# Attention heads taken in pairs: one step of lag, VectorE's divisions and maxima ahead of the weight split, and four biases with places of their own

## The chip, the cores and the metric

The kernel runs on one core of one Trainium2 chip. The metric is the device time of one execution in microseconds (us), given as the median over runs; one further execution was recorded by the profiler.

## The reference

One layer of a hybrid encoder over 512 tokens of width 2048, in float32: a combined input projection, three groups of mixers side by side (A: 8 heads of chunked attention with a relative bias, B: RWKV-7, C: 8 heads of sliding-window attention with sinks), an output projection, a cross-attention into 256 memory tokens, an MLP of width 8192, and a last norm. What the change touches are the attentions of A and C:

```python
logits = jnp.einsum('bcqhd,bckhd->bchqk', qc, kb).astype(jnp.float32) * (d ** -0.5)
logits = logits + bias[None, None]
logits = jnp.where(valid[None, :, None, None, :], logits, NEG_INF)
p = jax.nn.softmax(logits, axis=-1).astype(v.dtype)
o = jnp.einsum('bchqk,bckhd->bcqhd', p, vb)
```

In C the softmax has one more column, the sink of the head. The heads have 64 features, the chunks 64 tokens; A sees its own chunk and 8 before it (here: all earlier keys), C its own and one before it.

## The kernel before

Nearly all the work is a product of activations with weights on TensorE. Both sides are split into a high and a low part of type fp32r, and `split_mm` makes three products (L1176 to L1178) of each. A "unit" is two tiles of 128 rows of weights: SyncE loads it into one of four slots of `w_raw`, ScalarE copies it to `w_hi` (`hi_next`), VectorE subtracts to `w_lo` (`lo_next`, which raises `w_split`), and there are two slots of the split parts. So while TensorE works at unit n, ScalarE and VectorE make unit n + 1. A unit is 8 places of 3 products; `side(i)` puts other work of TensorE ahead of place i.

The attentions lie in the units v = 4 to 31 of three groups of products: the keys and values of the cross-attention (`G_XK`, `G_XV`, v = 0 to 15, products of 256 columns), and the part of the output projection that takes RWKV's output (`G_WR`, v = 16 to 31, 512 columns). The next group (`G_WA`, v = 32 on) takes the attentions' output and waits for all of it (`o_lo` of 8). At the end of v = 7, 15, 19, 23, 27 and 31 VectorE takes finished banks out of PSUM (`scaled_by_row`, `add_set`), and TensorE waits for it at the next unit.

Before, a unit of attention n (64 of them) is a tile t of two heads (t 0 to 3: A, t 4 to 7: C), one of its heads (`half`, features in partitions 0 to 63 or 64 to 127), and a block i of 128 queries. It has 128 (i + 1) keys in A and 128 or 256 in C: 136 blocks of 128 keys in all. It goes through a pipeline, one step each: TensorE makes the scores (L1386); VectorE adds the bias and takes the maximum (`sc_max`, L1000) and negates it (`sc_neg`, L1007 or L1010); ScalarE takes the exponential and its sum (`p_exp`, L610); VectorE divides (`p_ready`, L988 and L990); TensorE turns the blocks of 128 x 128 (`pT_mm`, L1395); ScalarE copies them to `att_pT` (`pT_ev`); TensorE multiplies with the values (`o_mm`, L1407). When the 8 units of a tile are done, ScalarE copies the tile (`o_hi`) and VectorE subtracts (`o_lo`, L1017). Scores, turning and outputs are products of type float32, which the profile shows as two passes each for scores and outputs.

Every engine runs the steps in one order written out by hand, and the units v say which steps are in each of them:

```python
def att_steps(v):
    if v < 4:
        return []
    steps_ = [2 * (v - 4) + i for i in range(2)] if v < 16 else [24 + 3 * (v - 16) + i for i in range(3)]
    return [st for st in steps_ if st < N_UNITS_ATT + 3]
```

GpSimd loads, in one order for all tiles, the queries and keys of a tile (`qk`), and the bias of each head n = 2t + half (L420), which it then masks with MEMSETs (`bias_ready`). Ahead of bias 1 it waits for the norm of the memory and loads RWKV's output `y_in` into h; ahead of bias 5 it waits until VectorE has split the eight tiles of `y_in` (`y_lo`, one in each unit v = 4 to 11, L1054), and then loads x into h, 1 MB at a time (L415).

Of the kernel before, what the change touches and what calls it, by code (L numbers as in the profile page):

```python
# [23 lines left out]
P = 128  # L24
# [3 lines left out]
L = 64  # L28
# [26 lines left out]
N_UNITS_ATT = 64  # L55
# [7 lines left out]
def hybrid_layer(nc, x, x_turned, mem_turned, gains, w_lora, w_pairs, w_rest, pair_prm, fin_prm, gup_tail, lora_mu,  # L63
                 a_line, c_line, sinks, norm_final, out):
    top = ExitStack()
    with top:
# [192 lines left out]
        def unit_of(n):  # L259
            t, half, i = n // 8, (n // 4) % 2, n % 4  # L260
            return (("A", t, half, i) + a_window(i)) if n < 32 else (("C", t, half, i) + c_window(i))
# [42 lines left out]
        def _(pool):  # L304
# [92 lines left out]
            for t in range(8):  # L397
                qt, kt = (t, 4 + t) if t < 4 else (A_TILES + t - 4, A_TILES + 4)
                if t >= 2:
                    pool.wait_ge(s["sc_mm"], 8 * (t - 1))  # L400
                pool.dma_start(qk[:, t % 2, 0, :], scr_qkv[qt // 3, qt % 3]).then_inc(s["qk_in"], 16)
                pool.dma_start(qk[:, t % 2, 1, :], scr_qkv[kt // 3, kt % 3]).then_inc(s["qk_in"], 16)
                for half in range(2):
# [16 lines left out]
                    pool.dma_start(bias[:, n % 2, 0:w], hankel).then_inc(s["bias_in"], 16)  # L420
                    pool.wait_ge(s["bias_in"], 16 * (n + 1))

                    step(nc.gpsimd.memset(bias[0:L, n % 2, 0:L], MASKED))
                    if t >= 4:
                        step(nc.gpsimd.memset(bias[0:L, n % 2, w - L:w], MASKED))
                        step(nc.gpsimd.memset(bias[L:P, n % 2, P:w], MASKED))
# [8 lines left out]
        def _(act):  # L435
# [152 lines left out]
            hi(0, UNITS * G_IN // RAW + 1, rest_slot(w_hi, 0), UNITS * G_IN)  # L588
            def att_step(st):
                n = st - 2  # L590
                if 0 <= n < N_UNITS_ATT:
                    keys = unit_of(n)[5]
                    act.wait_ge(s["pT_mm"], n + 1)
                    if n >= 2:
                        act.wait_ge(s["o_mm"], n - 1)
                    copy(att_pT[:, n % 2, 0:keys], ps[:, 6, 0:keys]).then_inc(s["pT_ev"], 1)
                n = st - 3
                if n >= 0 and n % 8 == 7:
                    t = n // 8
                    act.wait_ge(s["o_mm"], n + 1)  # L600
                    copy(act_hi[:, t if t < 4 else t + 8, :], bank(7)).then_inc(s["o_hi"], 1)
                n = st
                if n < N_UNITS_ATT:
                    kind, t, half, i, key0, keys = unit_of(n)
                    act.wait_ge(s["sc_neg"], n + 1)
                    if kind == "C":
                        head = (t - 4) + 4 * half
                        nc.scalar.activation(att_c[:, n % 4, 3:4], sink[:, head:head + 1], ACT.Exp,
                                             bias=att_c[:, n % 4, 1:2])
                    nc.scalar.activation(att_p[:, n % 4, 0:keys], att_p[:, n % 4, 0:keys], ACT.Exp,  # L610
                                         bias=att_c[:, n % 4, 1:2],
                                         accum_out=att_c[:, n % 4, 2:3]).then_inc(s["p_exp"], 1)
# [107 lines left out]
        def _(dve):  # L720
# [258 lines left out]

            def att_step(st):  # L980
                n = st - 1
                if 0 <= n < N_UNITS_ATT:
                    kind, keys = unit_of(n)[0], unit_of(n)[5]
                    dve.wait_ge(s["p_exp"], n + 1)
                    if kind == "C":
                        V.tensor_tensor(att_c[:, n % 4, 2:3], att_c[:, n % 4, 2:3], att_c[:, n % 4, 3:4], ALU.add)
                        dve.drain()
                    V.reciprocal(att_c[:, n % 4, 0:1], att_c[:, n % 4, 2:3])  # L988
                    dve.drain()
                    V.tensor_scalar(att_p[:, n % 4, 0:keys], att_p[:, n % 4, 0:keys], att_c[:, n % 4, 0:1], None,  # L990
                                    ALU.mult).then_inc(s["p_ready"], 1)
                n = st
                if n < N_UNITS_ATT:
                    kind, t, half, i, key0, keys = unit_of(n)
                    hd = n // 4
                    dve.wait_ge(s["sc_mm"], n + 1)
                    dve.wait_ge(s["bias_ready"], hd + 1)
                    if n >= 4:
                        dve.wait_ge(s["pT_mm"], n - 3)
                    V.tensor_tensor_reduce(out=att_p[:, n % 4, 0:keys], in0=ps[:, 4 + n % 2, 0:keys],  # L1000
                                           in1=falling(bias[:, hd % 2, 0:keys]), scale=1.0, scalar=-3e38,
                                           op0=ALU.add, op1=ALU.max,
                                           accum_out=att_c[:, n % 4, 0:1]).then_inc(s["sc_max"], 1)
                    dve.wait_ge(s["sc_max"], n + 1)
# [635 lines left out]
```

## Time and profile before

| | us |
|---|---|
| three runs, median (lowest to highest) | 2751.24 (2750.96 to 2754.89) |
| profiled execution, its time | 2754.32 |
| span of the profiled execution | 2752.6 |
| TensorE busy in it | 2715.1 |
| VectorE, ScalarE, GpSimd busy | 1238.5, 816.0, 133.6 |

The span goes from the first to the last instruction. "Busy" of TensorE counts matmuls from issue to a modelled end, so they overlap: of two that follow each other, the time between the starts is the cost, not the duration printed. TensorE's clock was granted at 0.997 of full on average.

### The profile page before, as it was taken

Reading aid. Unit: us, or ns where it says so; the run is one execution under the profiler, and the core shown is the slowest. Engines: PE = TensorE matmul, PEld = TensorE weight load, DVE = VectorE, ACT = ScalarE, POOL = GpSimd, SP = SyncE. Lnnn points to the kernel's source line nnn. Section 1 sums busy time; section 2 is a strip of 40 time slices with the busy share of each in tenths; the row PEclk is TensorE's granted clock in tenths of the full one; section 3 lists DMA queues with packets and bytes.
Section 4 is the critical chain, followed back from the end, with each engine's and each line's share of the span. In section 5 each row is a group of like instructions: output and inputs, shape, how many; then the busy total and the mean of one; then the engine's idle time right before and its main releaser. Section 6 shows DMA issues by size and latency. Waiting matters only on the chain.

```text
span 2752.6 us, 44358 instructions
## 1 busy us (share of the span) xinstructions
PE 2715.1 (99%) x18368; PEld 2159.3 (78%) x18368; DVE 1238.5 (45%) x1916; ACT 816.0 (30%) x1340; POOL 133.6 (5%) x237
## 2 busy tenths in 40 slices
PE   9999999999999999998999999999999999999997
PEld 7877777777777766786888888888888888888886
DVE  6266666666435545344433333333333333324334
ACT  5222222222125444344432222322222222122233
POOL 4000111001121100000000000000000000000000
PEclk9999999999999999999999999999999999999999
DMA  4311111111235521221223222222223222222232
GB/s 167 120 55 49 48 48 51 45 48 49 62 102 204 180 70 61 85 92 62 91 93 100 98 94 99 96 94 99 94 96 99 93 98 99 92 98 93 98 100 100
DMA packets 72403, 249.33 MB, mean 91 GB/s; under 512 B 8960, under 2 KB 9088, under 8 KB 71104
## 3 DMA queue, kind: packets, MB, share of 16 engines
q1 hardware_dynamic: 65232, 222.62, 24.6%
q0 software_dynamic: 7024, 24.56, 2.7%
q8 instruction: 115, 1.88, 0.3%
q14 instruction: 32, 0.26, 0.0%
HBM read 236.93 MB, written 10.22 MB: 90 GB/s over the span
## 4 chain that ended last, share of the span: by engine, by line
PE 97%; DVE 1%; ACT 1%; issue 0%; DMA 0%; DVEq 0%; ACTq 0%; SPq 0%
PE ps L1176 28%; PE ps L1178 26%; PE ps L1177 26%; PE ps L1194 9%; PE ps L1407 1%; PE ps L1386 1%; PE ps L1395 1%; PE ps L1188 1%; PE ps L1246 0%; PE ps L1243 0%; PE ps L1226 0%; PE ps L1237 0%; DVE w_lo L725 0%; PE ps L1252 0%; PE ps L1221 0%
## 5 line engine op out<-in xcount | busy, mean ns | idle before, releaser
L725 DVE TENSOR_TENSOR w_lo<-w_raw,w_hi 128x1024 fp32r<-128x1024 f32 (+2 forms) x440 | 505.9, 1150 | 1136.4 <-ACT w_hi L437 1136.3
L437 ACT ACTIVATE w_hi<-w_raw 128x1024 fp32r<-128x1024 f32 (+2 forms) x440 | 438.9, 998 | 1537.5 <-PE ps L1178 1537.1
L1176 PE MATMUL ps<-act_hi,w_hi 128*128 128x512 f32 x1792 | 730.5, 408 | 1.9 <-DVE w_lo L725 1.9
L1178 PE MATMUL ps<-act_hi,w_lo 128*128 128x512 f32 x1792 | 700.7, 391 | 0.0
L1177 PE MATMUL ps<-act_lo,w_hi 128*128 128x512 f32 x1792 | 700.1, 391 | 0.0
L1176 PE MATMUL ps<-w_hi,mid_hi 128*128 128x512 f32 x1088 | 425.1, 391 | 3.9 <-DVE w_lo L725 2.5
L1177 PE MATMUL ps<-w_lo,mid_hi 128*128 128x512 f32 x1088 | 424.0, 390 | 0.0
L1178 PE MATMUL ps<-w_hi,mid_lo 128*128 128x512 f32 x1088 | 423.9, 390 | 0.0
L1176 PEld LDWEIGHTS ps<-act_hi,w_hi 128*128 128x128 f32 x1792 | 336.5, 188 | 94.8 <-issue 12.1
L1178 PEld LDWEIGHTS ps<-act_hi,w_lo 128*128 128x128 f32 x1792 | 336.8, 188 | 72.3
L1177 PEld LDWEIGHTS ps<-act_lo,w_hi 128*128 128x128 f32 x1792 | 337.0, 188 | 69.2 <-issue 6.0
L1176 PEld LDWEIGHTS ps<-w_hi,mid_hi 128*128 128x128 f32 x1088 | 204.6, 188 | 46.6 <-DVE w_lo L725 2.9
L1178 PEld LDWEIGHTS ps<-w_hi,mid_lo 128*128 128x128 f32 x1088 | 204.6, 188 | 42.6
L1177 PEld LDWEIGHTS ps<-w_lo,mid_hi 128*128 128x128 f32 x1088 | 204.6, 188 | 42.0
L1030 DVE SCALAR_TENSOR_TENSOR h<-ps,rq,h 128x512 f32<-128x512 f32 x124 | 84.5, 743 | 96.4 <-PE ps L1178 96.4
L1176 PE MATMUL ps<-w_hi,act_hi 128*128 128x512 f32 x256 | 106.3, 415 | 4.2 <-DVE h L1024 3.6
L1178 PE MATMUL ps<-w_hi,act_lo 128*128 128x512 f32 x256 | 100.2, 392 | 0.0
L1177 PE MATMUL ps<-w_lo,act_hi 128*128 128x512 f32 x256 | 100.1, 391 | 0.0
L1176 PEld LDWEIGHTS ps<-w_hi,act_hi 128*128 128x128 f32 x256 | 48.0, 187 | 21.5 <-issue 13.3
L1178 PEld LDWEIGHTS ps<-w_hi,act_lo 128*128 128x128 f32 x256 | 48.0, 188 | 10.8
L1177 PEld LDWEIGHTS ps<-w_lo,act_hi 128*128 128x128 f32 x256 | 48.2, 188 | 8.1
L1176 PE MATMUL ps<-mid_hi,w_hi 128*128 128x256 f32 (+1 forms) x144 | 46.0, 319 | 3.3 <-DVE w_lo L725 2.7
(283 smaller groups left out, 2409.0 us busy)
## 6 DMA issues: line engine op xcount, KB each, us to landing
w_raw<-in_w_rest SPq DMA_DIRECT2D x320, 512.0 KB, 3.3
w_raw<-in_w_pairs SPq DMA_DIRECT2D x112, 384.0 KB, 3.0
x_t<-in_x_turned SPq DMA_DIRECT2D x8, 512.0 KB, 8.4
qk<-scr_qkv POOLq DMA_DIRECT2D x16, 256.0 KB, 3.1
h<-in_x POOLq DMA_DIRECT2D x4, 1024.0 KB, 11.4
out<-h SPq DMA_DIRECT2D x4, 1024.0 KB, 3.9
scr_qkv<-pad POOLq DMA_DIRECT2D x15, 256.0 KB, 4.1
w_raw<-in_w_lora SPq DMA_DIRECT2D x8, 288.0 KB, 7.3
```

Of the source, the lines that this page charges most:

```text
L437: return nc.scalar.activation(dst, src, ACT.Copy, scale=scale)
L725: V.tensor_tensor(dst, w_raw[:, slot, 0:dst.shape[-1]], high.bitcast(F32), ALU.subtract).then_inc(s["w_split"], 1)
L1030: V.scalar_tensor_tensor(dst, bank(4 * par + t), rq[:, 1, t:t + 1], dst, ALU.mult, ALU.add).then_inc(s["bank_evac"], 1)
L1176: mm(dst, a_hi, b_hi, start=start, stop=False)
L1177: mm(dst, a_hi, b_lo, start=False, stop=False)
L1178: return mm(dst, a_lo, b_hi, start=False, stop=stop)
L1188: last = nc.tensor.transpose(ps[:, turn_bank(k, kt), t * P:(t + 1) * P], h[:, t, kt * P:(kt + 1) * P], ident[:, :])
L1194: last = mm(dst[hf], lhsT[hf], rhs[hf], start=start, stop=stop)
L1386: mm(ps[:, 4 + n % 2, 0:keys], qk[hf, t % 2, 0, i * P:(i + 1) * P], qk[hf, t % 2, 1, key0:key0 + keys], start=True, stop=True).then_inc(s[ ...
L1395: last = nc.tensor.transpose(ps[:, 6, b * P:(b + 1) * P], att_p[:, n % 4, b * P:(b + 1) * P], ident[:, :])
L1407: last = mm(ps[HALF[half], 7, i * P:(i + 1) * P], vt[:, key0 // P + b, v0:v0 + L], att_pT[:, n % 2, b * P:(b + 1) * P], start=b == 0, stop ...
```

## The change

The unit of work is now a pair: the two heads of a tile for one block of queries, 32 of them, in 33 steps with one step of lag instead of three. In a step TensorE makes the scores of pair st and turns and multiplies pair st - 1, in four parts at four places of a unit. The two heads of the scores are issued one behind the other, on rows 0 to 63 and 64 to 127 of the array, into two banks; the outputs of the two heads take turns block by block, on columns 0 to 63 and 64 to 127. ScalarE takes exponentials of the new pair and copies of the old one in turn. VectorE does the divisions of the old pair and the maxima of the new pair, and in each unit the first step stands ahead of the split of the next unit. The biases 2 to 5 lie in h[:, 1], the biases 8, 9, 14 and 15 in `diag`, the others in `bias`; x's second block is loaded later, ahead of bias 8.

```diff
-            steps_ = [2 * (v - 4) + i for i in range(2)] if v < 16 else [24 + 3 * (v - 16) + i for i in range(3)]
-            return [st for st in steps_ if st < N_UNITS_ATT + 3]
+            steps_ = [v - 4] if v < 23 else [2 * v - 27, 2 * v - 26] if v < 28 else [v + 1]
+            return [st for st in steps_ if st <= ATT_PAIRS]
...
+        def bias_of(hd):
+            if hd < 8:
+                return bias[:, hd % 2, :] if hd // 2 in (0, 3) else h[:, 1, (hd - 2) * A_KEYS:(hd - 1) * A_KEYS]
+            near = diag[:, :, :].rearrange("p t n -> p (t n)") if hd // 2 in (4, 7) else bias[:, hd // 2 - 5, :]
+            return near[:, hd % 2 * C_KEYS:(hd % 2 + 1) * C_KEYS]
...
                     if n == 5:
                         pool.wait_ge(s["y_lo"], PAIRS)
                         pool.wait_ge(s["row_ready"], 2)
-                        for i in range(TT):
+                        for i in (0, 2, 3):
                             pool.dma_start(h[:, i, :], x[i * P:(i + 1) * P, :]).then_inc(s["h_in"], 16)
-                    if n >= 2:
-                        pool.wait_ge(s["sc_max"], 4 * (n - 1))
+                    if n == 8:
+                        pool.wait_ge(s["sc_max"], 24)
+                        pool.dma_start(h[:, 1, :], x[P:2 * P, :]).then_inc(s["h_in"], 16)
+                        pool.wait_ge(s["bank_evac"], 4 * (S_XV + 1))
+                    if t in (3, 5, 6, 7):
+                        pool.wait_ge(s["sc_max"], {3: 8, 5: 32, 6: 32, 7: 40}[t])
...
             def att_step(st):
+                for half in range(2):
+                    if st < ATT_PAIRS:
+                        att_exp(st, half)
+                    if st:
+                        att_turned(st - 1, half)
+                n = st - 1
+                if n >= 0 and n % 4 == 3:
+                    t = n // 4
                     act.wait_ge(s["o_mm"], n + 1)
                     copy(act_hi[:, t if t < 4 else t + 8, :], bank(7)).then_inc(s["o_hi"], 1)
...
             def att_step(st):
+                if st:
+                    for half in range(2):
+                        att_divide(st - 1, half)
+                if st < ATT_PAIRS:
+                    for half in range(2):
+                        att_max(st, half)
                 n = st - 1
+                if n >= 0 and n % 4 == 3:
+                    t = n // 4
                     mt = t if t < 4 else t + 8
                     dve.wait_ge(s["o_hi"], t + 1)
...
                     v = UNITS * (g - G_XK) + u
-                    lo_next(g, u)
+                    todo = att_steps(v) if g < G_WA else []
+                    for st in todo:
+                        att_step(st)
+                        if st == todo[0]:
+                            lo_next(g, u)
+                    if not todo:
+                        lo_next(g, u)
...
+                for half, hf in enumerate(HALF):
+                    last = mm(ps[:, 4 + half, 0:keys], qk[hf, t % 2, 0, i * P:(i + 1) * P],
+                              qk[hf, t % 2, 1, key0:key0 + keys], start=True, stop=True)
+                last.then_inc(s["sc_mm"], 1)
...
+                for b in range(nb):
+                    for half, hf in enumerate(HALF):
+                        v0 = t * P + half * L if kind == "A" else 512 + half * L
+                        last = mm(ps[hf, 7, i * P:(i + 1) * P], vt[:, key0 // P + b, v0:v0 + L],
+                                  att_pT[:, half, b * P:(b + 1) * P], start=b == 0, stop=b == nb - 1)
+                last.then_inc(s["o_mm"], 1)
...
-                        for j, st in enumerate(todo):
-                            if i == (8 * j + 4) // len(todo):
-                                att_step(st)
+                        if len(todo) == 1 and i % 2 == 1:
+                            att_part(todo[0], i // 2)
+                        elif len(todo) == 2:
+                            att_part(todo[i // 4], i % 4)
```

On TensorE, in the units of 256 columns, one place of a unit before held scores (L1386), turning (L1395) and outputs (L1407) of three units of attention in a row, between products of the weights:

```order
L1178 MATMUL ps<-mid_hi,w_lo 128x256
L1386 MATMUL ps<-qk 128x384
L1395 MATMUL ps<-ident,att_p 128x128
L1407 MATMUL ps<-att_pT,vt 64x128 x4
L1176 MATMUL ps<-mid_hi,w_hi 128x256
```

Of the change, the second turning and the outputs of a pair (L1419, L1432; the products are L1201 to L1203 there), at places 5 and 7 of a unit:

```order
L1419 MATMUL ps<-ident,att_p 128x128
L1201 MATMUL ps<-mid_hi,w_hi 128x256
L1202 MATMUL ps<-mid_lo,w_hi 128x256
L1203 MATMUL ps<-mid_hi,w_lo 128x256
L1201 MATMUL ps<-mid_hi,w_hi 128x256
L1202 MATMUL ps<-mid_lo,w_hi 128x256
L1203 MATMUL ps<-mid_hi,w_lo 128x256
L1432 MATMUL ps<-att_pT,vt 64x128 x2
L1201 MATMUL ps<-mid_hi,w_hi 128x256
```

Each part now stands alone between products, and only one place of three products is left behind the outputs in a unit.

On VectorE, before, at the end of the first tile of heads, in unit 9 (`w_lo` is the split, L1054 the split of `y_in`, L1017 the low part of the tile's output):

```order
L725 TENSOR_TENSOR w_lo<-w_raw,w_hi 128x1024
L1054 TENSOR_TENSOR act_lo<-h,act_hi 128x512
L988 RECIPROCAL att_c<-att_c 128x1
L990 TENSOR_SCALAR att_p<-att_p,att_c 128x256
L1000 ISA att_p,att_c<-ps,bias 128x384
L1000 ISA att_c 128x1
L1010 TENSOR_SCALAR att_c<-att_c 128x1
L1017 TENSOR_TENSOR act_lo<-ps,act_hi 128x512
```

Of the change, at the end of the same tile, in unit 8 (L1015 and L1024 are maximum and negation, L1038 the low part of the output, L742 the split, L1081 that of `y_in`):

```order
L1005 TENSOR_SCALAR att_p<-att_p,att_c 128x512
L1015 ISA att_p,att_c<-ps,h 128x128
L1015 ISA att_c 128x1
L1024 TENSOR_SCALAR att_c<-att_c 128x1
L1015 ISA att_p,att_c<-ps,h 128x128
L1015 ISA att_c 128x1
L1024 TENSOR_SCALAR att_c<-att_c 128x1
L1038 TENSOR_TENSOR act_lo<-ps,act_hi 128x512
L742 TENSOR_TENSOR w_lo<-w_raw,w_hi 128x1024
L1081 TENSOR_TENSOR act_lo<-h,act_hi 128x512
```

The split has moved from the head of a unit to behind the tile's output.

On GpSimd, before, biases 4 and 5 and the loads of x between them:

```order
L401 DMA qk<-scr_qkv 128x512
L402 DMA qk<-scr_qkv 128x512
L420 DMA bias<-in_a_line 128x512
L423 MEMSET bias 64x64
L415 DMA h<-in_x 128x2048 x4
L420 DMA bias<-in_a_line 128x512
L423 MEMSET bias 64x64
```

Of the change, the same place:

```order
L410 DMA qk<-scr_qkv 128x512
L411 DMA qk<-scr_qkv 128x512
L433 DMA h<-in_a_line 128x512
L436 MEMSET h 64x64
L424 DMA h<-in_x 128x2048 x3
L433 DMA h<-in_a_line 128x512
L436 MEMSET h 64x64
```

Bias 5 (the second of tile t = 2) keeps its place behind the loads of x, of which there are three instead of four. Its first use was step 20, in unit 14; by pairs it is step 8, in unit 12.

## Rows read from the trace of the kernel before

**Rows 1.** The page: busy us, share of the span, number of instructions.

```profile
PE 2715.1 (99%) x18368; PEld 2159.3 (78%) x18368; DVE 1238.5 (45%) x1916; ACT 816.0 (30%) x1340; POOL 133.6 (5%) x237
```

**Rows 2.** Windows: stretch, length, busy of each engine, granted clock, DMA share, GB/s.

```profile
873.20:1121.49 248.29, 242.01 (x1207) 165.22 (x1206) 128.07 (x418) 108.56 (x270) 21.58 (x61) 1.00 0.31 102
```

**Rows 3.** Timeline of TensorE: start, duration, engine, line, operation, count.

```profile
906.97 0.91 PE L1386 MATMUL ps<-qk 64*128 64x384 f32 x2
907.81 0.33 PE L1395 MATMUL ps<-ident,att_p 128*128 128x128 f32 x1
908.07 1.09 PE L1407 MATMUL ps<-att_pT,vt 128*64 128x128 f32 x8
909.09 0.38 PE L1176 MATMUL ps<-mid_hi,w_hi 128*128 128x256 f32 x1
...
909.55 0.28 PE L1176 MATMUL ps<-mid_hi,w_hi 128*128 128x256 f32 x1
...
968.30 1.12 PE L1386 MATMUL ps<-qk 64*128 64x512 f32 x2
969.35 0.44 PE L1395 MATMUL ps<-ident,att_p 128*128 128x128 f32 x2
969.72 0.43 PE L1407 MATMUL ps<-att_pT,vt 128*64 128x128 f32 x2
970.08 0.50 PE L1176 MATMUL ps<-w_hi,act_hi 128*128 128x512 f32 x1
```

**Rows 4.** Timeline of TensorE, two products of 64 rows (RWKV's part).

```profile
141.12 0.39 PE L1178 MATMUL ps<-act_hi,w_lo 128*128 128x512 f32 x1
141.44 0.69 PE L1221 MATMUL ps<-lora,prm 64*128 64x512 f32 x1
141.45 0.69 PE L1222 MATMUL ps<-lora,prm 64*128 64x512 f32 x1
141.98 0.59 PE L1221 MATMUL ps<-lora,prm 64*128 64x512 f32 x1
...
142.50 0.50 PE L1176 MATMUL ps<-act_hi,w_hi 128*128 128x512 f32 x1
142.84 0.39 PE L1177 MATMUL ps<-act_lo,w_hi 128*128 128x512 f32 x1
```

**Rows 5.** Timeline of TensorE, four turned blocks alone between products.

```profile
1175.89 0.40 PE L1178 MATMUL ps<-w_hi,act_lo 128*128 128x512 f32 x1
1176.13 0.60 PE L1188 MATMUL ps<-ident,h 128*128 128x128 f32 x4
...
1176.80 0.39 PE L1177 MATMUL ps<-w_lo,act_hi 128*128 128x512 f32 x1
```

**Rows 6.** Timeline of VectorE: the split, a maximum and its negation, a tile's low part.

```profile
921.39 1.23 DVE L725 TENSOR_TENSOR w_lo<-w_raw,w_hi 128x1024 fp32r<-128x1024 f32 x1 [2.26 <-ACT w_hi L437]
...
923.64 0.55 DVE L1000 CUSTOM_DVE_ANT_0 att_p<-ps,bias 128x384 f32<-128x384 f32 x1
...
924.23 0.15 DVE L1010 TENSOR_SCALAR att_c<-att_c 128x1 f32<-128x1 f32 x1
...
937.58 0.69 DVE L1017 TENSOR_TENSOR act_lo<-ps,act_hi 128x512 fp32r<-128x512 f32 x1
```

**Rows 7.** Groups by line, ScalarE, 860 to 1120: busy, mean ns, idle before.

```profile
L437 ACT ACTIVATE act_hi<-ps 128x512 fp32r<-128x512 f32 x8 | 4.8, 599 | 6.1 <-PE ps L1407 6.1
```

**Rows 8.** Timeline of GpSimd, and the landing of its x loads.

```profile
923.51 2.12 POOL L415 DMA_DIRECT2D h<-in_x  x4 [6.31 <-DVE act_lo L1054]
...
941.64 0.15 POOL L423 MEMSET bias<- 64x64 f32 x1 [14.35 <-DMA bias<-in_a_line]
...
DMA to landing us min/median/max: 7.8/11.4/15.7
```

**Rows 9.** Windows, columns as in rows 2, about TensorE's gap ahead of unit 0.

```profile
854.48:857.15 2.67, 0.00 (x1) 0.03 (x1) 2.34 (x4) 2.00 (x2) 2.67 (x6) 1.00 0.73 233
857.50:861.50 4.00, 4.00 (x24) 4.00 (x23) 0.53 (x1) 0.70 (x1) 1.10 (x3) 0.57 0.94 338
```

More of the change, by code:

```diff
@@ L588, in _, with att_turned @@
             hi(0, UNITS * G_IN // RAW + 1, rest_slot(w_hi, 0), UNITS * G_IN)
-            def att_step(st):
[L590 to L599, printed above, removed]
+            def att_turned(n, half):
+                keys = unit_of(n)[4]
+                act.wait_ge(s["pT_mm"], 2 * n + half + 1)
+                if n:
+                    act.wait_ge(s["o_mm"], n)
+                copy(att_pT[:, half, 0:keys], ps[:, 6, 0:keys]).then_inc(s["pT_ev"], 1)
@@ new lines, in att_exp @@
+            def att_exp(n, half):
+                kind, t, i, key0, keys = unit_of(n)
+                j = slot_of(n, half)
+                act.wait_ge(s["sc_neg"], 2 * n + half + 1)
+                if kind == "C":
+                    head = (t - 4) + 4 * half
+                    nc.scalar.activation(att_c[:, j, 3:4], sink[:, head:head + 1], ACT.Exp, bias=att_c[:, j, 1:2])
+                nc.scalar.activation(att_p[:, j, 0:keys], att_p[:, j, 0:keys], ACT.Exp, bias=att_c[:, j, 1:2],
+                                     accum_out=att_c[:, j, 2:3]).then_inc(s["p_exp"], 1)
@@ L603, in att_step @@
[L603 to L612, printed above, removed]
@@ L978, in _ @@
             lo(UNITS * G_IN, 0, rest_slot(w_lo, 0), rest_slot(w_hi, 0))
-            def att_step(st):
-                n = st - 1
[L982 to L1004, printed above, removed]
-                    if kind == "C":
-                        head = (t - 4) + 4 * half
-                        V.tensor_scalar(att_c[:, n % 4, 1:2], att_c[:, n % 4, 0:1], sink[:, head:head + 1], -1.0,
-                                        ALU.max, ALU.mult).then_inc(s["sc_neg"], 1)
-                    else:
-                        V.tensor_scalar(att_c[:, n % 4, 1:2], att_c[:, n % 4, 0:1], -1.0, None,
-                                        ALU.mult).then_inc(s["sc_neg"], 1)
-                n = st - 3
-                if n >= 0 and n % 8 == 7:
-                    t = n // 8
@@ new lines, in att_turn @@
+            def att_turn(n, half):
+                keys = unit_of(n)[4]
+                pe.wait_ge(s["p_ready"], 2 * n + half + 1)
+                if 2 * n + half:
+                    pe.wait_ge(s["pT_ev"], 2 * n + half)
+                for b in range(keys // P):
+                    last = nc.tensor.transpose(ps[:, 6, b * P:(b + 1) * P],
+                                               att_p[:, slot_of(n, half), b * P:(b + 1) * P], ident[:, :])
+                last.then_inc(s["pT_mm"], 1)
@@ new lines, in att_out @@
+            def att_out(n):
+                kind, t, i, key0, keys = unit_of(n)
+                pe.wait_ge(s["pT_ev"], 2 * n + 2)
+                if n % 4 == 0 and t:
+                    pe.wait_ge(s["o_lo"], t)
+                nb = keys // P
+                for b in range(nb):
[4 more added lines that the diff above has]
+                last.then_inc(s["o_mm"], 1)
@@ L1412, in rest_unit, with att_part @@
+            def att_part(st, part_):
+                if part_ == 0 and st < ATT_PAIRS:
+                    att_scores(st)
+                elif part_ in (1, 2) and st:
+                    att_turn(st - 1, part_ - 1)
+                elif part_ == 3 and st:
+                    att_out(st - 1)
             def rest_unit(n, u, stationary, a_hi, a_lo, kts, cols, par, first, last_kt, reused, side=None, turned_out=None):
```

91 lines of the change are left out of this document (45 added, 46 removed).

## The prediction

> **What bounds the kernel now.** I read the page first: TensorE is busy for 99% of the span [rows 1], so only work taken off TensorE, or waits of TensorE, can move the end. Then the windows answer for the stretch of the attentions, units 4 to 31, from the first score to the first product of the stage behind: 248.3 us, TensorE busy 242.0, idle 6.3, clock at full, VectorE busy 128 and ScalarE 109 of it [rows 2]. So VectorE and ScalarE have room on average, and the rest is read unit by unit. The timeline of TensorE in two units [rows 3] gives the parts of an attention step. Scores of 512 keys take 1.05 us to the next start, of 384 keys 0.84: 0.21 per 128 keys and 0.20 fixed. Turning a block costs 0.11 (0.26 for one, 0.37 for two) and 0.15 fixed. The outputs cost 0.11 per pass, two passes per block (1.02 for eight passes, 0.36 for two), and 0.14 fixed. What the products lose at the two ends of such a group is seen at [rows 4]: 0.32 instead of 0.23 ahead of it and 0.34 instead of 0.23 behind it, 0.20 together.
>
> **The change, part by part.** *Work on TensorE.* The 64 units of before have 136 blocks of 128 keys. Now each unit costs 0.20 + 0.15 + 0.14 + 0.20 = 0.69 fixed and 0.21 + 0.11 + 0.21 = 0.53 per block: 64 x 0.69 + 136 x 0.53 = 44 + 73 = 117 us.
>
> The change issues the scores of two heads back to back, one on rows 0 to 63 of the array and one on 64 to 127. The trace has this very shape: L1221 and L1222 start at 141.44 and 141.45, again at 141.98, and the four passes of 512 columns end after 1.06 us [rows 4], as long as two passes of one head take now (1.05). So a pair of scores costs what one costs. The scores stand alone between products, so a pair pays 0.20 + 0.20 fixed. The turned blocks are as many, but stand alone too: four of them between two products (1175.89, 1176.13, 1176.80) stretch 0.91 - 0.45 = 0.46, 0.11 each with nothing fixed [rows 5]. The outputs of a pair go to columns 0 to 63 and 64 to 127, with different moving data. No row shows that form. Bounds: overlapped fully, 0.21 per block of the pair; not at all, 0.42. I take full overlap, because its nearest row is the row pair [rows 4], also two halves of the array with two moving operands; fixed 0.14 + 0.20.
>
> New sum, 32 pairs with 68 blocks: fixed 32 x (0.40 + 0.34) = 24, per block 0.21 + 0.22 + 0.21 = 0.64, 44 us: 68. TensorE loses 117 - 68 = 49 us of work (35 if the outputs don't overlap).
>
> The Trainium skill, "TensorE: Matmul & The Clock Gate", "Measured speedup vs the span model", gives 2.38x for three column tiles, below the factor 3; an estimate by that, 1.6x for two tiles, would cost 3 to 4 us of the 49. The same page says in "The mechanism" that matmuls start and end in strict order; with both passes of one half ahead of the other half's that would be three slots for a pair of scores instead of two, 7 us more. The rows show two slots [rows 4], so I leave it out.
>
> *The order on VectorE: the split waits for the output of a tile.* The next unit's `w_lo` now stands behind all of the first step of a unit. In a plain unit this is hidden: with scores three products into the unit (0.4 us) and ready 0.9 later, two maxima at 0.75 each (923.64 to the end of 924.23's row, 0.74 [rows 6]) and `w_lo` (1.2 [rows 6]) end at about 4.1, while the shortest unit lasts 24 products x 0.12 (0.36 for three: 0.46 from 909.09 to 909.55, less the 0.10 behind a group [rows 3]) + 0.74 + one to four blocks, 4.5 to 6.5. Margin 0.4 to 2.
>
> But at a step that ends a tile (st a multiple of 4) VectorE first waits for `o_hi`, which waits for the outputs, and these are issued at place 7 of 8, ahead of the unit's last three products. From the start of the outputs of four blocks: 0.85 + 0.30 to their end, ScalarE's copy 0.60 [rows 7], `act_lo` 0.6 to the next start and `w_lo` 1.23 [rows 6], with hand-overs of 0.1: 3.7 us. TensorE in that time has 0.85 + 0.34 + 0.36 = 1.55. So TensorE waits 2.1 us. That is at units 8 and 12; with three products of 512 columns (0.69) it is 1.8 at units 16 and 20. In units 23, 25 and 27 the ending step is the second of the unit, behind the split, and only delays the adding of the set by 0.3. At unit 31 `o_lo`, then the split, then the first addition to h stand in a row: 2.4 us, 1.5 more than now. Sum 8 + 2 = 10 us.
>
> *The order on GpSimd: bias 5 behind x.* This is the largest term. The four biases let 2, 3 and 4 be loaded early, but bias 5 (heads counted as n = 2t + half) still stands behind the wait for all eight `y_lo` and behind the loads of x. Now it is needed at unit 14; by pairs it is needed at step 8, unit 12, and the eighth `y_lo` is done in unit 11. Now the x loads start at 923.51, bias 5 is there at 941.64 after a wait of 14.35, and the four x loads land 7.8 to 15.7 us after their issue, in steps of 3 us: the third so at about 937.5 [rows 8], the bias some 0.8 behind it, 0.1 to 0.2 more for its masking. With three loads ahead, bias 5 comes about 14.5 us after their start. `y_lo` ends about 1.1 us before unit 12 begins (unit 11: split done at 4.4, then 0.7, of 6.2). So bias 5 is there 13.4 us into unit 12. VectorE's second maximum waits for it, ScalarE's second exponential for that, and the copy of the second turned half (and so TensorE's outputs at place 7) stands behind that exponential: 13.4 + 0.5 + 0.5 + 0.5 = 14.9 against 4.1 without it. TensorE waits 10.8 us. Bounds: nothing, if the bias passed the x loads; 13, if it came with the end of four (18.1 us).
>
> *Chain of a step.* Half 1 is turned when ScalarE has copied half 0, six products earlier. Copies of three or four blocks (0.5 to 0.6) and an exponential ahead of them make waits of 0.1 to 0.3 at about twelve pairs and about 1 at the four where steps follow in a two-step unit or first meet 512 keys: 7 us, an estimate, against 1.5 to 2 of the 6.3 now; the rest of those stays (evacuated banks). Bounds 2 and 12.
>
> *The clock.* Behind a gap of 2.67 us (TensorE busy 0.00 from 854.48 to 857.15) the mean granted clock of 857.5 to 861.5 is 0.57 [rows 9]: between the two levels, 1.2 and 2.4 GHz, that is 3.4 us at the lower one, 1.7 us lost. The gap of 11 us will surely do that, for 2.5 us with the wait behind it; of the five of about 2 us I count one or two, 2.5 us. Bounds 2 and 11.
>
> Sum: -49 + 10 + 11 + 5 + 5 = -18 us. Terms rounded the other way (117.7 - 69.2 = 48.5, 34 - 6.7 = 27.3 of waits) give -16; I take -17. The profiled execution took 2754.3 us, 3.1 above the median of the three runs, so 2737.3 there and 2734 for the median.
>
> **The rivals.**
> *A. The outputs don't overlap by columns.* For it: no row has the form, and both halves need all 128 rows. Against: [rows 4]. It gives 14 us back: 2748, no change that can be told. Chance 0.17. The change not doing what it says (pairs one after another) ends at the same place.
> *B. The bias is no wait.* For it: three loads may land much faster than four did, if the split weights ask for less at that time. Against: it waited 14.35 us in just this place [rows 8]. 11 + 2.5 us less: 2721. Chance 0.12.
> *C. Slower: the split is late in every plain unit.* VectorE's `w_lo` ends at 4.1 into units of 4.5 and up. If the divisions at the head wait for the last exponential, each microsecond beyond the margin costs TensorE a microsecond per unit. There are 23 such units; with a mean margin of 1.5 (more in the units of 512 columns) the kernel is slower than before by more than 0.2% from 2.5 us of delay per unit on, since 17 + 5.5 us over 23 units is 1.0 beyond the margin. For it: margins of 0.4 and 1 in units 4 and 5. Against: VectorE has 5 us of work in a unit of 6.5 and more. At 1.1 us per unit: -17 + 25 = +8, 2759. Chance 0.09.
>
> **How the numbers follow.** Forecast, between 2727 and 2743: 0.60. A 0.17, B 0.12, C 0.09, elsewhere 0.02. A measurement of this kernel tells 0.2%, 5.5 us, from no change. Faster: forecast 0.60, B 0.12 and a small part of A 0.03, in all 0.75. Same: the rest of A, 0.14. Slower: C and the rest, 0.11. The range goes down past B's 2721 by 3 us of a cheaper clock, 2718, and up past A's 2748 to 2750; C lies outside. The forecast's own range, 2727 to 2743, is its sum with the bounds of chain and clock.
>
> **What would show it.** Right: score pairs starting together, with as much time as one; outputs of a pair at 0.21 per block; one TensorE gap of about 11 us near 60 us after the first score, with GpSimd waiting for the bias; gaps of 1.8 to 2.4 behind `act_lo` at the ends of tiles 0, 1, 2, 3 and 7; the stretch from first score to the next stage near 230 us instead of 248. Wrong: outputs at 0.42 per block, no gap at bias 5, or `w_lo` ending behind TensorE in units that end no tile.

## The result, and the profile after

The changed kernel takes 2736.73 us (median of 5 runs, 2734.98 to 2740.60), the kernel before 2752.57 beside it: a ratio of 0.9944, 95% interval [0.9934, 0.9955]. That is 0.56% faster; forecast were 2734 us, from 2718 to 2750, and faster. One of the five executions of the kernel before took 4457.83 us and the other four 2750.96 to 2754.89, with a median of 2751.91, so the gain is 15 to 16 us. The profiled execution took 2739.77 us, 3.0 above the median, with a span of 2738.0.

TensorE is still the bound. The page has it busy for 37.5 us less than in [rows 1], though the span is only 14.6 us shorter, so waits have come in (busy us, share of the span, instructions):

```profile
PE 2677.6 (98%) x18368; PEld 2139.4 (78%) x18368; DVE 1235.5 (45%) x1916; ACT 811.9 (30%) x1340; POOL 133.0 (5%) x237
```

The windows answer for the stretch from the first score to the next stage, and for three pieces of it (busy us of PE, PEld, DVE, ACT and POOL with instructions, granted clock, DMA share, GB/s):

```profile
871.57:1107.01 235.44, 205.17 (x1206) 145.66 (x1206) 125.11 (x418) 104.59 (x270) 20.62 (x60) 0.94 0.33 104
...
920.00:940.00 20.00, 8.14 (x50) 6.26 (x48) 3.47 (x12) 3.41 (x8) 2.42 (x6) 0.62 0.60 223
940.00:1000.00 60.00, 56.24 (x336) 40.76 (x335) 29.25 (x91) 25.20 (x59) 6.93 (x22) 0.98 0.36 110
1000.00:1105.00 105.00, 96.56 (x492) 62.95 (x492) 56.27 (x210) 45.03 (x138) 6.23 (x20) 0.97 0.23 71
```

Beside [rows 2] the stretch is 12.9 us shorter by the windows and 12.4 from the first score's own start (247.8 before, 235.4 now). TensorE's busy time fell from 242.0 to 205.2, its idle time rose from 6.3 to 30, and its clock is no longer full. What it waits for stands in the list of TensorE's waits over the whole execution (us in total, times, longest), with four of its lines. Of the first, 4 waits and 6.9 us lie in the stretch, behind tiles 0 to 3; the other three lines lie in it altogether:

```profile
PE ps L1201 <- DVE w_lo L742: 12.9, 7, 2.7
PE ps L1432 <- ACT att_pT L450: 10.2, 1, 10.2
...
PE ps L1201 <- DVE h L1045: 5.0, 4, 2.4
PE ps L1419 <- ACT att_pT L450: 5.0, 11, 1.3
```

The 10.2 us are bias 5. GpSimd's timeline shows the three x loads, the bias load behind them, and 11.43 us until that has landed; TensorE's shows the gap, which ends 61 us after the first score (start, us, engine, line, operation, count, idle time before it and what ended it):

```profile
917.30 1.61 POOL L424 DMA_DIRECT2D h<-in_x  x3 [23.19 <-DVE act_lo L1081]
918.90 0.54 POOL L433 DMA_DIRECT2D h<-in_a_line  x1
930.88 0.14 POOL L436 MEMSET h<- 64x64 f32 x1 [11.43 <-DMA h<-in_a_line]
...
932.75 1.98 PE L1432 MATMUL ps<-att_pT,vt 128*64 128x128 f32 x16 [10.17 <-ACT att_pT L450]
```

The bias is there 13.6 us after the x loads' start. The outputs behind the gap last 1.98 us, against 1.09 for the same 16 passes at 997.92: the clock is at its lower level there.

The other new gap stands at the end of a tile. The timeline of all engines at the end of tile 0 (unit 8):

```profile
897.82 0.60 ACT L450 ACTIVATE act_hi<-ps 128x512 fp32r<-128x512 f32 x1 [1.19 <-PE ps L1432]
...
898.45 0.69 DVE L1038 TENSOR_TENSOR act_lo<-ps,act_hi 128x512 fp32r<-128x512 f32 x1 [3.40 <-ACT act_hi L450]
899.06 1.22 DVE L742 TENSOR_TENSOR w_lo<-w_raw,w_hi 128x1024 fp32r<-128x1024 f32 x1
...
900.33 0.39 PE L1201 MATMUL ps<-mid_hi,w_hi 128*128 128x256 f32 x1 [2.00 <-DVE w_lo L742]
```

From the last line up: TensorE has waited 2.00 us for the split, the split started when VectorE had the tile's low part, and VectorE had stood 3.40 us waiting for ScalarE's copy of the outputs, which came only after the outputs themselves.

**The balance of the stretch.** I counted TensorE's time from each start to the next, idle time left out, by line. Scores went from 41.9 to 22.2 us, turned blocks from 24.2 to 10.4, outputs from 39.0 to 20.8: 51.7 less. The weight products between them went from 136.5 to 152.2, 15.7 more. Marked gaps went from 6.3 to 29.8, 23.5 more. Together -12.5 (-12.4 before rounding). The 15.7 us in the products are more interesting than they look, since the trace calls them busy; the last two experiments take them apart.

### The profile page after: what moved, and what is told of

It is laid out like the page before. It is cut to its first block, busy times and chain, and to the rows that moved or that the text cites. A ratio compares the mean times of both kernels' runs of the same rounds, so it can differ in the third digit from the quotient of the medians.

```text
span 2738.0 us, 44362 instructions
## 1 busy us (share of the span) xinstructions
PE 2677.6 (98%) x18368; PEld 2139.4 (78%) x18368; DVE 1235.5 (45%) x1916; ACT 811.9 (30%) x1340; POOL 133.0 (5%) x237
## 4 chain that ended last, share of the span: by engine, by line
PE 94%; DVE 2%; ACT 1%; DMA 1%; issue 1%; DVEq 0%; POOL 0%; ACTq 0%; SPq 0%; POOLq 0%
PE ps L1201 28%; PE ps L1203 26%; PE ps L1202 26%; PE ps L1219 9%; PE ps L1432 1%; PE ps L1409 1%; PE ps L1419 1%; DMA h<-in_mem_turned 1%; PE ps L1213 1%; DMA h<-in_a_line 0%; DVE w_lo L742 0%; PE ps L1271 0%; PE ps L1262 0%; PE ps L1268 0%; PE ps L1251 0%
## 5 line engine op out<-in xcount | busy, mean ns | idle before, releaser
L742 DVE TENSOR_TENSOR w_lo<-w_raw,w_hi 128x1024 fp32r<-128x1024 f32 (+2 forms) x440 | 505.6, 1150 | 1076.0 <-ACT w_hi L450 1075.9
L1201 PE MATMUL ps<-act_hi,w_hi 128*128 128x512 f32 x1792 | 730.0, 407 | 0.8 <-DVE w_lo L742 0.8
L1203 PE MATMUL ps<-act_hi,w_lo 128*128 128x512 f32 x1792 | 700.0, 391 | 0.0
L1201 PE MATMUL ps<-w_hi,mid_hi 128*128 128x512 f32 x1088 | 425.3, 391 | 3.9 <-DVE w_lo L742 2.5
L1203 PE MATMUL ps<-w_hi,mid_lo 128*128 128x512 f32 x1088 | 423.8, 390 | 0.0
L1201 PEld LDWEIGHTS ps<-act_hi,w_hi 128*128 128x128 f32 x1792 | 336.1, 188 | 93.6 <-issue 12.1
L1203 PEld LDWEIGHTS ps<-act_hi,w_lo 128*128 128x128 f32 x1792 | 336.5, 188 | 72.2
L1201 PEld LDWEIGHTS ps<-w_hi,mid_hi 128*128 128x128 f32 x1088 | 204.6, 188 | 46.5 <-DVE w_lo L742 2.9
L1203 PEld LDWEIGHTS ps<-w_hi,mid_lo 128*128 128x128 f32 x1088 | 204.5, 188 | 42.7
L1201 PE MATMUL ps<-w_hi,act_hi 128*128 128x512 f32 x256 | 110.9, 433 | 8.9 <-DVE h L1045 5.0
L1203 PE MATMUL ps<-w_hi,act_lo 128*128 128x512 f32 x256 | 101.3, 396 | 0.0
L1201 PEld LDWEIGHTS ps<-w_hi,act_hi 128*128 128x128 f32 x256 | 48.8, 190 | 28.2 <-issue 15.7
L1203 PEld LDWEIGHTS ps<-w_hi,act_lo 128*128 128x128 f32 x256 | 48.8, 190 | 11.0
L1201 PE MATMUL ps<-mid_hi,w_hi 128*128 128x256 f32 (+1 forms) x144 | 49.5, 344 | 6.9 <-DVE w_lo L742 6.3
```

The source lines that it names most:

```text
L742: V.tensor_tensor(dst, w_raw[:, slot, 0:dst.shape[-1]], high.bitcast(F32), ALU.subtract).then_inc(s["w_split"], 1)
L1201: mm(dst, a_hi, b_hi, start=start, stop=False)
L1203: return mm(dst, a_lo, b_hi, start=False, stop=stop)
```

## The experiments

**1. Bias 5 ahead of the x loads.** GpSimd waits for `y_lo` and loads x one bias later.

```diff
-                    if n == 5:
+                    if n == 6:
                         pool.wait_ge(s["y_lo"], PAIRS)
```

> Bias 5 is loaded ahead of x's blocks 0, 2 and 3 instead of behind them; all else as in the change. My account (TensorE's gap of 10.2 us ahead of the outputs of pair 7 is the wait for bias 5, and the low clock behind it costs 3 us more): the gap is gone, the clock stays at full after unit 12, 12 to 13 us less than the change, near 2724 us. Rival (the gap is DMA traffic as such: any load at that time collides with the 3 MB of x): bias 6 or the queries and keys of tile 3, now behind x, are late instead, and a gap of 5 us or more stands near unit 16; at most 6 us less.

Measured: 2726.64 us (2725.83 to 2737.03), ratio 0.9902 [0.9885, 0.9919]: 10.1 us faster than the change, where 12 to 13 were expected and the rival allowed 6. The outputs' wait is gone from the list and no bias is late. But the clock did not stay at full: the profiled execution took 2737.03 us, 10 more than the other three, and no marked wait explains that. Its mean granted clock is 0.991, that of the other three 0.995 to 0.996. In its stretch the clock is low at the end of or behind each of the four gaps for `w_lo` and behind gaps of 1.51 and 1.30 us (1028.2), and once more right behind the stretch. Four windows of it:

```profile
870.00:920.00 50.00, 45.80 (x331) 37.37 (x330) 34.44 (x99) 30.46 (x66) 4.32 (x11) 0.93 0.42 135
920.00:940.00 20.00, 17.92 (x123) 14.58 (x122) 9.54 (x35) 8.46 (x20) 3.00 (x7) 0.83 0.71 263
940.00:1000.00 60.00, 54.64 (x303) 38.40 (x303) 29.83 (x91) 23.37 (x53) 6.84 (x21) 0.95 0.33 106
1000.00:1105.00 105.00, 96.26 (x489) 62.93 (x488) 55.96 (x202) 44.15 (x134) 6.58 (x21) 0.96 0.23 71
```

**2. The split ahead of a tile's low part.** VectorE issues `lo_next` before the part of a step that waits for `o_hi`.

```diff
                         att_step(st)
                         if st == todo[0]:
                             lo_next(g, u)
+                        att_tile_end(st)
```

> VectorE's low part of a finished tile (the wait for ScalarE's copy of it) is moved behind the next unit's split; maxima and divisions stay ahead of the split. My account: the waits of TensorE for w_lo of 2.0, 1.6, 1.7 and 1.7 us behind tiles 0 to 3 are gone, the one at unit 32 falls from 2.4 to about 1.3, and the low clock behind the 2.0 us gap (1.7 us) is gone: 8 to 9 us less than the change, near 2728 us. Rival (the split is late because of maxima and divisions ahead of it): the gaps stay above 1 us, 0 to 3 us less.

Measured: 2731.69 us (2728.59 to 2734.92), ratio 0.9920 [0.9904, 0.9937], 5.0 us faster than the change, not 8 to 9. The `w_lo` gaps at units 8, 12, 16 and 20 are gone and unit 32's is 1.22 instead of 2.36. Instead 0.81 us appear ahead of a turning, and the bias gap stays at 9.8. The cause of the waits is shown, and in the profiled execution so is their worth: its stretch is 9.9 us shorter than the change's (225.6 against 235.4), 7.7 of it marked gaps. Behind the stretch, where the two kernels are the same, it took 2.4 us longer, with a piece of low clock at 1266.5 that the change's profile has not.

**3. Both.**

> Both of the edits of the two runs ahead of this one. If the two waits are separate, the gains add up: 20 to 22 us less than the change, near 2716 us. If they share a cause, less than 16 us.

Measured: 2719.07 us (2713.23 to 2719.36), ratio 0.9876 [0.9859, 0.9892], 17.7 us faster than the change. Expected were 20 to 22 for separate waits and less than 16 for a shared cause, so the size lies between the two; but the single gains add up to 15.1, and both together gain no less than that, so the two waits are separate costs. The profiled execution was the fastest of the four, 2713.23. Its stretch, in the windows answer:

```profile
869.89:1081.98 212.09, 199.40 (x1207) 141.27 (x1206) 124.94 (x418) 104.24 (x270) 20.79 (x60) 0.98 0.37 118
```

**4. Outputs of the two heads one after the other**, all blocks of one half of the array's columns, then all of the other.

```diff
-                for b in range(nb):
-                    for half, hf in enumerate(HALF):
+                for half, hf in enumerate(HALF):
+                    for b in range(nb):
```

> The change, but the outputs of a pair are issued all blocks of the first head, then all of the second, so that two column halves are not in use at once except at the boundary. If the halves overlap by columns in the change: outputs of four blocks take near 1.9 us instead of 1.03, of two near 1.0 instead of 0.59, 0.21 us per block of a pair more, 68 blocks, up to 14 us in all (2749 us). If the saving came from fewer switches alone: no change.

Measured: 2740.94 us (2739.66 to 2744.84), ratio 0.9960 [0.9946, 0.9974], only 4.2 us slower than the change, where overlap alone was expected to cost up to 14. The outputs of two blocks still take 0.59 us, as in turn; three take 1.07 instead of 0.81, four 1.51 instead of 1.03. So this issue order keeps the halves apart only in part, and this run did not tell what overlap is worth. Numbers 6 and 7 do.

**5. The split ahead of the whole step**, the opposite of the change's order on VectorE.

```diff
-                    for st in todo:
-                        att_step(st)
-                        if st == todo[0]:
-                            lo_next(g, u)
-                    if not todo:
-                        lo_next(g, u)
+                    lo_next(g, u)
+                    for st in todo:
+                        att_step(st)
```

> The change with one part undone: in every unit VectorE makes the next unit's split first, as the kernel before does, and the divisions and maxima of the pair behind it. My account of why that order is there: with one step of lag the divisions must be done before place 3 of the unit, and the split waits for ScalarE's part, so TensorE would wait about 1 us at the turning of nearly every pair: 25 to 32 us more than the change, near 2765 us, slower than the kernel before; the gaps behind w_lo vanish. Rival (the order costs nothing but the gaps behind w_lo): 5 to 8 us less than the change.

Measured: 2777.00 us (2774.48 to 2778.43), ratio 1.0093 [1.0076, 1.0109]: 40 us slower than the change, more than the 25 to 32 expected, and slower than the kernel before. In the profile the stretch is 32.8 us longer than the change's, 24.5 of it marked gaps. TensorE's waits over the whole execution:

```profile
PE ps L1416 <- ACT att_pT L450: 22.4, 26, 1.4
PE ps L1416 <- DVE att_p L1005: 22.4, 23, 2.6
PE ps L1198 <- DVE w_lo L742: 7.0, 3, 2.7
```

The gaps for `w_lo` in the stretch are gone (the 7.0 lie outside it), and turnings wait instead, for divisions and copies. The lag of one step needs the divisions first; the split behind them makes no gap for `w_lo` where no tile ends, as the change and number 2 show.

**6 and 7. No overlap at all.** Number 6 takes experiment 4's loops and writes both heads' outputs to the same 64 columns; number 7 computes both score tiles on the same 64 rows.

```diff
-                        last = mm(ps[hf, 7, i * P:(i + 1) * P], vt[:, key0 // P + b, v0:v0 + L],
+                        last = mm(ps[HALF[0], 7, i * P:(i + 1) * P], vt[:, key0 // P + b, v0:v0 + L],
```

```diff
-                    last = mm(ps[:, 4 + half, 0:keys], qk[hf, t % 2, 0, i * P:(i + 1) * P],
-                              qk[hf, t % 2, 1, key0:key0 + keys], start=True, stop=True)
+                    last = mm(ps[:, 4 + half, 0:keys], qk[HALF[0], t % 2, 0, i * P:(i + 1) * P],
+                              qk[HALF[0], t % 2, 1, key0:key0 + keys], start=True, stop=True)
```

> The outputs of both heads of a pair go to columns 0 to 63 and the same place in PSUM, one head behind the other, so no two column halves can be in use at once; the second half of each attention output tile is not computed. If columns overlap in the change: outputs of two blocks take 1.0 us instead of 0.59, of four 1.9 instead of 1.03; 13 to 15 us more than the change, near 2751 us. If what mattered was the fewer switches: no more than 3 us.

> The scores of both heads of a pair are taken from the rows 0 to 63 (the first head's queries and keys twice; the second head's scores are not computed), so the two can't use two halves of the rows at once. If rows overlap in the change: a pair of scores of 512 keys takes 1.9 us instead of 1.06, of 256 keys 1.06 instead of 0.63; 13 to 15 us more than the change, near 2751 us, less where the gaps were. Rival: TensorE would overlap them whatever rows they use: no more than 3 us.

Measured: 2757.57 us (2754.61 to 2761.03, ratio 1.0017 [1.0007, 1.0027]) and 2757.08 (2754.83 to 2763.50, ratio 1.0019 [1.0010, 1.0029]): 20.8 and 20.4 us slower than the change. Each alone takes back the whole gain. TensorE's timeline, four blocks of outputs and the next product, in the change, in number 4 and in number 6:

```profile
997.92 1.09 PE L1432 MATMUL ps<-att_pT,vt 128*64 128x128 f32 x16
998.94 0.50 PE L1201 MATMUL ps<-w_hi,act_hi 128*128 128x512 f32 x1
```

```profile
999.99 1.58 PE L1432 MATMUL ps<-att_pT,vt 128*64 128x128 f32 x16
1001.50 0.50 PE L1201 MATMUL ps<-w_hi,act_hi 128*128 128x512 f32 x1
```

```profile
1008.70 1.96 PE L1432 MATMUL ps<-att_pT,vt 128*64 128x128 f32 x16
1010.59 0.50 PE L1201 MATMUL ps<-w_hi,act_hi 128*128 128x512 f32 x1
```

From start to next start 1.02, 1.51 and 1.89 us. One to four blocks take 0.37, 0.59, 0.81 and 1.03 in the change, 0.58, 1.02, 1.45 and 1.89 in number 6: 0.22 against 0.435 per block. And the scores of 512 keys in the change and in number 7, 1.06 against 1.91 to the next start:

```profile
982.47 1.13 PE L1409 MATMUL ps<-qk 64*128 64x512 f32 x4
983.53 0.50 PE L1201 MATMUL ps<-w_hi,act_hi 128*128 128x512 f32 x1
```

```profile
993.45 1.98 PE L1409 MATMUL ps<-qk 64*128 64x512 f32 x4
995.36 0.50 PE L1201 MATMUL ps<-w_hi,act_hi 128*128 128x512 f32 x1
```

By these rows 68 blocks times 0.21 are 14 to 15 us for either. Counted over the stretch of the profiled executions, from start to next start, the outputs take 15.7 us more in number 6 (36.5 against 20.8) and the scores 16.1 more in number 7 (38.3 against 22.2), part of them at a low clock. The stretches are 17.3 and 15.3 us longer than the change's; the rest is products, 2.9 and 2.4 longer, and marked gaps, 1.5 and 3.3 shorter. The mean clock of the stretch is 0.93 in both, against 0.94 in the change. So most of the distance between 14 and the 20 us of the medians is not in the groups: it is clock, and the place of the profiled executions among the others (the change's lies 3.0 us above its median, number 7's 2.3 below).

**8. The bias gap filled** with 40 products of a unit matrix, so that TensorE works through it.

```diff
+                if n == 7:
+                    for _ in range(40):
+                        mm(ps[:, 7, i * P:(i + 1) * P], ident[:, :], ident[:, :], start=True, stop=True)
                 pe.wait_ge(s["pT_ev"], 2 * n + 2)
```

> The change, with 40 products of 128 x 128 (float32, about 8.6 us, into a part of the bank that is overwritten after) put where TensorE waits for bias 5 in unit 12, ahead of the outputs of pair 7. If the gap is what lowers the clock and the low clock is what costs: the clock stays at full behind it and the kernel is 2 to 3 us faster than the change, though TensorE does more work. If the clock has another cause, or its price is hidden: no change; if the gap had gone for another reason than bias 5, 8 us slower.

Measured: 2736.25 us (2735.16 to 2738.53), ratio 0.9941 [0.9925, 0.9958], no gain over the change. Its timeline of TensorE:

```profile
930.98 1.09 PE L1435 MATMUL ps<-att_pT,vt 128*64 128x128 f32 x16 [0.97 <-ACT att_pT L450]
932.00 0.39 PE L1201 MATMUL ps<-mid_hi,w_hi 128*128 128x256 f32 x1
...
934.63 0.58 PE L1201 MATMUL ps<-mid_hi,w_hi 128*128 128x256 f32 x1 [2.00 <-DVE w_lo L742]
```

The clock stays full through the gap (the product behind the outputs lasts 0.39), but then the next gap is 2.00 us long instead of 1.61, and the clock is low behind that (0.58 for the same kind of product). Over the profiled stretch the low clock costs 5.2 us against 7.9 in the change, by the count given below, and the clock is low once more right behind the stretch, at 1104.4, where the change has it full. So most of the loss moved; on the medians nothing was gained.

**9 and 10. The copy of a turned half ahead of the exponential.** In the profile of the change, products just ahead of a second turning take longer than their neighbours, without a mark. The timeline at one of them:

```profile
881.99 0.28 PE L1202 MATMUL ps<-mid_lo,w_hi 128*128 128x256 f32 x1
...
882.01 0.36 ACT L450 ACTIVATE att_pT<-ps 128x256 f32<-128x256 f32 x1
...
882.10 0.28 PE L1203 MATMUL ps<-mid_hi,w_lo 128*128 128x256 f32 x1
...
882.51 0.41 PE L1419 MATMUL ps<-ident,att_p 128*128 128x128 f32 x2
```

Products of 256 columns start 0.12 apart; here 0.41 pass from 882.10 to the turned blocks. ScalarE's copy of the first half ends at 882.37, and the second half may be turned only then. ScalarE could have copied at about 881.75, an estimate from the first half's turning (881.30, 0.38 long), but did an exponential first. The edit, in experiment 3's kernel (9) and alone (10):

```diff
+                    if st:
+                        att_turned(st - 1, half)
                     if st < ATT_PAIRS:
                         att_exp(st, half)
-                    if st:
-                        att_turned(st - 1, half)
```

> This is the version with bias 5 ahead of the x loads and the split ahead of a tile's low part (2719.07 us), and in it ScalarE copies a turned half ahead of the new step's exponential instead of behind it. Theory: what the chain of a step costs beyond the waits that the trace marks is a wait of the second turning for the copy of the first half. In that version the products ahead of 24 of the 64 turnings take 0.08 to 0.41 us longer to the next start, 5.7 us together, and the trace marks 6.9 us more as waits. The copy starts right behind an exponential (882.01, with the blocks turned at about 881.7), so with the copy first both should go in the units of one step: the products ahead of a turning then take 0.23 or 0.12 to the next start throughout, and the kernel is 5 to 8 us shorter, near 2713. Rival 1: the lengthened products are a fixed cost of turning blocks between products; then only marked waits go, 2 us or less, near 2717. Rival 2, slower: the exponentials come 0.3 us later, the second maximum's row with them, and the next division and split; then new waits for w_lo or att_p appear and the time is 2722 or more.

> The change (2736.7 us) with the same edit alone: ScalarE copies a turned half ahead of the new step's exponential. Theory: the same 5 to 8 us go, near 2730; the waits for w_lo at the ends of tiles and the 10 us for bias 5 stay. Rival 1 (fixed cost of turning): near 2735. Rival 2 (late exponentials): 2739 or more.

Measured: number 9 takes 2707.34 us (2706.20 to 2710.28), ratio 0.9834 [0.9821, 0.9848], 11.7 less than number 3; number 10 takes 2731.55 (2726.43 to 2733.96), ratio 0.9922 [0.9909, 0.9936], 5.2 less than the change. In number 9 the same product is followed after 0.14 us (TensorE's timeline), and the stretch is 10.2 us shorter than in number 3 (windows):

```profile
881.73 0.28 PE L1206 MATMUL ps<-mid_hi,w_lo 128*128 128x256 f32 x1
881.87 0.41 PE L1422 MATMUL ps<-ident,att_p 128*128 128x128 f32 x2
```

```profile
871.32:1073.23 201.91, 194.45 (x1206) 140.19 (x1206) 125.94 (x418) 103.89 (x270) 20.73 (x60) 1.00 0.38 124
```

Of the 10.2, 4.7 are marked gaps (12.0 to 7.3) and 5.5 time that the trace called work: 2.7 of unmarked waits ahead of turnings, and 2.8 of low clock, which number 3 has from 1007.4 to 1014.2 behind a gap of 1.49 us. Number 9 has a gap of 1.50 at the same place (1004.08) and its clock stays full. The theory holds against the rival of a fixed cost: without the clock the edit is worth 7.4 us, inside the 5 to 8 expected, and the 11.7 of the medians hold the clock besides (mean 0.995 in the three executions of number 3 near 2719, 0.995 to 0.998 in number 9's). In number 10 the bias gap takes in some of the gain: it is now 11.48 us long and ends with `w_lo`. Its profiled execution was the fastest of its five, so its stretch (11.8 us shorter than the change's) is no measure of the edit; but no marked wait of a second turning is left in it, where the change has 5.0 us. Number 9 is the fastest version of the study, 1.66% faster than the kernel before.

## Why the prediction was right, and where it was off

The sum was -18, taken as -17, and the measurement is -15 to -16 us on the medians. In the profiled executions it is -14.6, and 2.1 of these lie ahead of the first score, where the two kernels are the same: it stands at 873.7 in the kernel before and at 871.6 in the change, and at 869.9 to 873.4 in the ten other versions, which are the same up to there too. In the stretch -12.4 stand against the forecast's -18. By its terms:

- **Work on TensorE, -49: right.** (By its own figures the two sums are 116.2 and 67.2 instead of 117 and 68; the difference is the same.) Number 9 has no low clock and few unmarked waits left, and there scores, turnings, outputs and products together take 194.6 us against 241.5, 46.9 less; about 1.4 us of unmarked waits are still in it (products ahead of turnings, 0.03 to 0.23 each). That gives 48 to 49. The pair of scores costs what one cost (1.06 against 1.05 at 512 keys), the outputs overlap fully, the turned blocks cost 0.11 each and nothing fixed where they don't wait. The overlap is shown by taking it away, in number 6 for the outputs, which refutes rival A, and in number 7 for the scores. What the turned blocks save by standing alone is read from rows; no run puts them back. The Trainium skill, "TensorE: Matmul & The Clock Gate", "Measured speedup vs the span model", gives 2.38x for three column tiles; the prediction's estimate from it would have taken 3 to 4 us of the gain. The trace does not agree: 0.22 against 0.435 per block is a factor of 1.98, and no loss is seen.
- **The split behind a tile's output, +10: 8.4** (2.00, 1.61, 1.66 and 1.65, and at unit 32, where the wait is for h, 2.36 instead of 0.87), in the places forecast. About 1 us more stands unmarked in the products at these gaps: where the clock is full, the one ahead of a gap takes 0.17 us longer than in number 9, without the gap, and the one behind it 0.10. Number 2 shows the cause.
- **Bias 5, +11: 10.2**, 13.6 us after the x loads' start instead of 14.5. Number 1 shows the cause, and rival B is refuted. (The bound of 13 for the end of four loads is 14.4 by the prediction's own working.)
- **The chain of a step, +5: mis-sized, 8.4.** Marked waits for `att_p` and `att_pT` rose by 4.9 us without the bias. But another 3.5 stand in 21 products ahead of second turnings, where nothing marks them, 0.08 to 0.29 each. The step had the mechanism ("Half 1 is turned when ScalarE has copied half 0", with "an exponential ahead of them") and counted it for about twelve pairs at 0.1 to 0.3 and four at about 1; 21 pairs wait, 10 of them without a mark. Number 10, the edit of ScalarE's order alone, takes away all 5.0 us of marked waits ahead of second turnings and 2.5 of the 3.5.
- **The clock, +5: mis-sized, 7.9.** It is low four times in the stretch: behind the 2.00 us gap of unit 8 (901.0 to 904.4), in and behind the bias gap (924.8 to 941.9), behind a gap of 1.65 (1003.4 to 1006.8) and behind gaps of 1.50 and 1.30 (1034.1 to 1037.5). The same instructions stand in number 9 at full clock; from start to next start they take 1.3, 3.6, 1.6 and 1.5 us longer in the change. The forecast had only the bias gap and one or two of the others. This is read from one execution, 3 us above the median, and numbers 1 and 8 show that another one loses at other gaps.

These terms give -48.5 + 8.4 + 1 + 10.2 + 8.4 + 7.9 = -12.6; counted were -12.4 to -12.5. So the path, the waits and their places were right. Chain and clock were each some 3 us too small, the split and the bias together 1 to 2 too large, and the time ahead of the first score, which is luck, hides 2 us of the difference in the total. Of the second sum in the prediction, the 34 and 6.7 stand in no row. Rival C did not occur: in the change `w_lo` is late only where a tile ends. Number 5 shows that a slower kernel was near all the same, by the other order of the same instructions.

Open is the clock. It differs between executions of one kernel, and no run here holds it fixed; so each comparison carries some us of it, and what one gap costs in clock can't be told from its length.

## What to carry to other kernels

When a change takes work off the engine that bounds the kernel, the next cost is in the order of the others: list for each of them what stands ahead of the instruction that the bound engine now reaches sooner, a large transfer ahead of a small one that is needed at once above all. Here three edits of order, without any arithmetic changed, were worth 29 us behind a change that brought 16. And count from start to start, not only marked gaps: a wait shorter than the tail of the instruction before it shows as a long instruction.

## What the runs showed of the hardware

- Two heads' outputs overlap by halves of the array's columns even when they aren't issued in turn: with all of one half first, two, three and four blocks take 0.59, 1.07 and 1.51 us, which is 0.43, 0.38 and 0.38 less than on the same columns. In the four blocks of number 4 that start at 999.99, the fifth of the first half's eight passes starts at 1000.48 and the second half's first at 1000.49, and two streams of starts, each 0.11 apart, run side by side until the eight are through. So about four passes of 0.11 run beside others, for two blocks as for four. The Trainium skill, "TensorE: Matmul & The Clock Gate", "The mechanism", has matmuls start and end in strict order; worked out by that rule, an estimate, about one pass, 0.11, could overlap here, and the trace does not agree.
- The clock fell behind gaps of 1.3 to 2.0 us in some executions and stayed full behind gaps of the same length in others. One kernel (number 1) took 2725.8 to 2726.7 us three times, with a mean granted clock of 0.995 to 0.996, and 2737.0 once, with 0.991.
- With a gap filled with products of a unit matrix the clock stayed full there, and it fell behind the next gap (number 8).
- A load of 256 KB queued behind three of 1024 KB landed 11.9 us after its issue (918.90, used from 930.88 on), with the three ahead of it issued from 917.30 on. Another of 256 KB, issued at 932.66 behind two of 256 KB, was used 5.2 us later (937.82).
